# Scores of a pair of heads on the two row halves of TensorE, issued together every second step

## The reference

```
h = rmsnorm(x); proj = h @ w_in
# group A: 8 heads, 2 kv heads, window 128, a learned sink per head
s = einsum(q, k) * 64 ** -0.5;  s = where(0 <= qpos - kpos < 128, s, -inf)
p = softmax(concat(s, sink))[..., :-1];  o_A = p @ v
# group B: 8 heads, 2 kv heads: compressed + selected + window branch, each with its own K/V
o_B = g0 * o_cmp + g1 * o_sel + g2 * o_win
x = x + concat(o_A, o_B) @ w_out
x = x + peer_ffn(rmsnorm(x));   y = rmsnorm(x)
```

## Time and profile before

| | |
|---|---|
| median of three runs | 1526.71 us |
| the profiled execution | 1529.9 us, of which its span (first to last instruction) 1528.0 us |
| attention stage, first scores to last values | 114.8 to 249.7 us |
| TensorE's mean granted clock over the span | 0.997 of full speed |

### The profile page before, as it was taken

One profiled execution on the slowest core, in us unless ns is written; L12 is line 12 of the kernel. 1 busy time (PEld: TensorE's weight loads), 2 busy tenths in 40 slices (PEclk: granted clock), 3 DMA queues, 4 the chain that ended last, 5 costly groups with the idle time before them and its releaser, 6 DMA issues.

```text
span 1528.0 us, 22468 instructions
## 1 busy us (share of the span) xinstructions
PE 1503.2 (98%) x8379; PEld 1345.0 (88%) x8379; DVE 1226.5 (80%) x2329; ACT 629.1 (41%) x1050; POOL 534.3 (35%) x357
## 2 busy tenths in 40 slices
PE   9999999999999999999999999999999999999997
PEld 6888888889899999998888888999999999999996
DVE  5577885449999999975776776888888889888885
ACT  6247675332222356663333333333333333333335
POOL 0323102055755710002111112555555556555530
PEclk9999999999999999999999999999999999999999
DMA  8302003323323668889999989999999999999971
GB/s 313 146 25 87 1 2 128 117 89 112 131 60 114 173 208 307 320 307 368 299 309 301 302 293 339 363 367 370 356 361 370 362 371 361 369 367 356 371 254 69
DMA packets 148507, 378.94 MB, mean 248 GB/s; under 512 B 11792, under 2 KB 76688, under 8 KB 145456
## 3 DMA queue, kind: packets, MB, share of 16 engines
q1 hardware_dynamic: 100400, 201.84, 38.3%
q0 software_dynamic: 37200, 138.56, 24.5%
q10 hardware_dynamic: 10800, 37.11, 6.6%
HBM read 338.60 MB, written 38.86 MB: 247 GB/s over the span
## 4 chain that ended last, share of the span: by engine, by line
PE 85%; DVE 10%; DMA 2%; ACT 1%; issue 1%; SPq 0%; DVEq 0%; ACTq 0%
PE bank L1898 22%; PE bank L1803 20%; PE bank L1524 12%; PE bank L1904 11%; PE bank L1812 10%; PE bank L1735 2%; DVE oh L1406 2%; DVE gp L1414 2%; DVE gp L1411 2%; DVE oh L1409 2%; PE bank L1719 1%; DVE d_lo L1395 1%; DMA w_raw<-wts 1%; PE bank L1644 1%; PE bank L1821 1%
## 5 line engine op out<-in xcount | busy, mean ns | idle before, releaser
L1803 PE MATMUL bank<-h_hi,d_hi 128*128 128x384 f32 x1024 | 349.2, 341 | 1.1 <-DVE h_lo L1260 1.1
L1803 PE MATMUL bank<-h_lo,d_hi 128*128 128x384 f32 x1024 | 344.9, 337 | 0.0
L582 POOL DMA_INDIRECT p_in<-rows,p_row x128 | 160.5, 1254 | 403.7 <-DVE p_dot L1433 186.0
L582 POOL DMA_INDIRECT p_in<-up,p_row x128 | 172.0, 1344 | 191.5 <-DVE p_dot L1433 97.1
L1812 PE MATMUL bank<-h_hi,d_lo 128*128 128x384 f32 x1024 | 200.2, 338 | 0.0
L1803 PEld LDWEIGHTS bank<-h_hi,d_hi 128*128 128x128 f32 x1024 | 192.5, 188 | 4.0 <-issue 1.3
L1803 PEld LDWEIGHTS bank<-h_lo,d_hi 128*128 128x128 f32 x1024 | 192.4, 188 | 3.2
L1898 PE MATMUL bank<-u_hi,w_hi_e 128*128 128x512 f32 x750 | 192.2, 392 | 1.3 <-DVE w_lo_e L1458 1.3
L1898 PE MATMUL bank<-u_hi,w_lo_e 128*128 128x512 f32 x750 | 191.0, 390 | 0.0
L1904 PE MATMUL bank<-u_lo,w_hi_e 128*128 128x512 f32 x750 | 190.8, 390 | 0.0
L1812 PEld LDWEIGHTS bank<-h_hi,d_lo 128*128 128x128 f32 x1024 | 180.8, 188 | 0.0
(11 more groups left out here) (290 smaller groups left out, 2438.8 us busy)
## 6 DMA issues: line engine op xcount, KB each, us to landing
d_raw<-down SPq DMA_DIRECT2D x128, 512.0 KB, 5.7
u_raw<-up SPq DMA_DIRECT2D x128, 512.0 KB
gates_dram<-ev ACTq DMA_DIRECT2D x12, 2048.0 KB, 6.7
g_e<-gates_dram SPq DMA_DIRECT2D x32, 768.0 KB
w_raw<-wts SPq DMA_DIRECT2D x9, 2048.0 KB, 8.3
act_dram<-f_act ACTq DMA_DIRECT2D x59, 192.0 KB
a_e<-act_dram SPq DMA_DIRECT2D x59, 192.0 KB
xt<-x_in SPq DMA_DIRECT2D x2, 2048.0 KB, 11.1
```

The lines of the kernel that those rows point to most:

```text
L582: pool.indirect_dma_start(out=p_in[n % GR][:], out_offset=None, in_=rows if kind == "D" else up.rearrange("n p d -> (n p) d"), in_offset=b ...
L1803: nc.tensor.matmul(bank[6 + e % 2][:, 0:TD], d_hi[e % DH_R][:, k], h[:, k, 0:TD], start=(k == j == 0), stop=False)
```

## The change

Three things change, in one loop of PE and in the order of heads.

1. **Row halves.** A score matmul of up to 256 keys takes only its group's 64 rows of query and key tile (`own`): rows 0 to 63 for group 0, rows 64 to 127 for group 1. In the compiled program these 64 instructions are then placed on a tile of 64 x 128 of the array, 32 of them at row 0 and 32 at row 64. The number of instructions stays the same, and so do the wide scores' operands.
2. **Order of heads.** `UNITS` lists heads 0, 4, 1, 5, 2, 6, 3, 7, so that units 2p and 2p + 1 are the same `j` of both groups. `nmax` and `rsum` keep their columns by head (`column(s)`), so that the sinks and gates still match.
3. **Two at a time.** PE calls `query_keys` for s and s + 1 in even steps, for all widths, and for none in odd steps.

```diff
-UNITS = [(qb, br, h) for qb in range(TB) for br in (SWA, SEL, WIN) for h in range(HEADS)]
+PAIRED = [g * HPG + j for j in range(HPG) for g in range(GROUPS)]
+UNITS = [(qb, br, h) for qb in range(TB) for br in (SWA, SEL, WIN) for h in PAIRED]
+
+
+def column(s):
+
+    return s // HEADS * HEADS + UNITS[s][2]
...
-                                         bias=nmax[:, s:s + 1], accum_out=rsum[:, s:s + 1])\
+                                         bias=nmax[:, column(s):column(s) + 1], accum_out=rsum[:, column(s):column(s) + 1])\
...
-                elif br == SWA:
-                    q = (q_g1 if g else qT)[:, 0, j, tok]
-                else:
-                    q = q_g1[:, 1, j, tok] if g else q_g0[:, j, tok]
+                own = slice(DH * g, DH * g + DH)
+                if br == SWA:
+                    q = (q_g1 if g else qT)[own, 0, j, tok]
+                elif n <= PACKED:
+                    q = q_g1[own, 1, j, tok] if g else q_g0[own, j, tok]
                 if s >= 3:
                     pe.wait_ge(S("max_done"), s - 2)
...
-                    m = nc.tensor.matmul(bank[s % 3][:, 0:n], q, kT[:, K_OF[br], k0:k0 + n], start=True, stop=True)
+                    m = nc.tensor.matmul(bank[s % 3][:, 0:n], q, kT[own, K_OF[br], k0:k0 + n], start=True, stop=True)
...
-                    query_keys(s)
+                    if s % GROUPS == 0:
+                        for u in range(s, s + GROUPS):
+                            query_keys(u)
```

More of the change, by code:

```diff
@@ L1172, in _ @@
                                            scalar=nsink[:, h:h + 1] if br == SWA else -NEG,
-                                           op0=ALU.add, op1=ALU.min, accum_out=nmax[:, s:s + 1])\
+                                           op0=ALU.add, op1=ALU.min, accum_out=nmax[:, column(s):column(s) + 1])\
                      .then_inc(S("max_done"), 1)
@@ L1726, in _ @@
                     gi = u // HEADS
-                    if uh == 0 and gi >= 2:
+                    if u % HEADS == 0 and gi >= 2:
                         pe.wait_ge(S("o_free"), gi - 1)
-                    if uh == 0 and gi == 1:
+                    if u % HEADS == 0 and gi == 1:
                         pe.wait_ge(S("gexp_done"), TB)
```

## The result

Five runs of the changed kernel took 1532.69, 1552.95, 1553.55, 1554.24 and 1554.87 us, median 1553.55, against 1526.71 for the kernel before. The ratio, over runs of both kernels, is 1.0152 (95% interval 1.0108 to 1.0196). The interval is wide because the kernel has two lengths; the profile shown first is of the short one, 1532.69 us, and a second one of 1550 us was taken later.

What follows compares the result with a forecast made beforehand. PE was taken to bound the 137 to 216 us stretch, with DVE close beside it. 16 pairs x 0.20 us, half lost to DVE in eight, give 2.4: 1526.7 - 2.4 = 1524.3 us, full range 1519.8 to 1530.3.

Steps and rivals of the forecast that it cites:

- The pair: 256-key scores of two heads, 137.4 to 215.9 us: side by side, 0.78 us with tile changes against 0.98, 0.20 less.
- The sum: 16 pairs on the path x 0.20 = 3.2 us, cut for DVE to 2.4 us less; 128-key scores gain nothing.
- half of eight pairs: About 8 of 16 pairs lie in or beside 148.2 to 167.6 us, DVE 90% full; they keep 0.10 us each.
- The even step's added wait: PE waits for the maximum of unit s - 2; 0 to 0.4 us per stall, taken as offset by earlier odd-head scores.
- the clock rival: Half-filled arrays and gaps make PE's clock fall once more under PE-bound steps: 1527.7 us, twice 1531.1; chance 0.06.
- such a stretch: 6.8 us at 0.50 of full clock, as from 119.0 to 125.8 us before, doing 3.4 us of work.
- the signs of being wrong: Four records one after another, step pair under 1.9 us, `max_done` stalls before even scores, or clock falling outside 119 to 126 us.

Runs made afterwards that it cites:

- order_only: The changed kernel with full 128-row score matmuls again, keeping pairs and head order; 1524.87 us, ratio 0.9988 to the kernel before.
- fill_start_after: The changed kernel plus six full-array 512-column matmuls in PE's pauses of steps 3 to 5; median 1545.27 us over eleven runs.
- rows_256: The changed kernel with half rows only for 256-key scores, 128-key scores on full rows; two groups, 1523.47 to 1524.71 and 1534.10 to 1536.25 us, ratio 1.0009.
- pause_tiles: Paired order, full-row scores, ten ACT copies pausing PE, and a 64-row matmul of 16 keys ahead of each short pair; 1565.70 us.

## Why the prediction was wrong

- **The pair: right.** Two steps at 2.01 us (forecast 2.00) and the halves side by side. Held against order_only's rows, the changes of tile show on both sides: 0.48 us instead of 0.40 from the values to the pair and 0.28 instead of 0.21 from the transposes to the values, so with the 0.63 us of the pair itself 0.78, as forecast. Here the Trainium skill's rule that matmuls start strictly in program order (TensorE: Matmul & The Clock Gate, part 3) does not hold across row halves, by the four rows above, if each record is an instruction. With its rule on draining at a change of tiling mode (TensorEngine Tiling (Array Packing), Key Properties) the 0.08 and 0.07 us above agree.
- **The sum: near in total, wrong in its parts.** With no fall the changed kernel takes 1523.99 and 1524.91 us (two runs of fill_start_after, with its six added matmuls), 2.3 and 1.4 less than the kernel before in the same series; forecast 2.4 less. That the total comes near is partly luck. For 1.8 us come from the paired order, which I had put at nothing, and some 0.5 from the half rows, which I had put at 2.4 (the runs at 0.998 and above have a median of 1524.4 us in order_only and 1524.0 in rows_256, which is within their spread). Paired, full rows need 2.15 us for two steps, not 2.20, so half rows have only 0.14 us a pair to give; and DVE's waits for these scores fell from 7.1 us to 2.9 by the order alone:

```profile
DVE pr L1179 <- PE bank L1653: 2.9, 6, 0.7
```

And of these 0.14 us a pair most turned into waiting, less for DVE, to which the forecast gave half of eight pairs, than for ACT's exponentials ahead of the transposes. (In fill_start_after DVE is busy 17.30 of the 19.40 us from 148.2 to 167.6, 89%; over 90% was forecast.) Between 137.4 and 215.9 us this wait is, in order_only and then in rows_256:

```profile
PEld bank L1730 <- ACT pr L772: 4.3, 7, 1.2
PEld bank L1730 <- ACT pr L772: 8.2, 16, 1.2
```

- **The even step's added wait: no cost found.** With full rows that order is faster than the one before.
- **The step that failed: the clock rival.** I had named half-filled arrays and gaps at this place, and gave them 0.06 and the price of "such a stretch", once or twice: 1527.7 or 1531.1. But I had the clock fall once more, and in both profiles of the changed kernel it fell once, where it had before, and stayed down. I took the length of 6.8 us at half clock for a property of the clock. It depends on the work that follows: back after 7 us with full rows, after 31 and 79 us in the two profiles of the changed kernel, and 82 us after PE resumed where it was made to pause. The price of one such microsecond was 0.28 to 0.34 us, less than the 0.5 that I had used, but there were 30.7 and 78.5 of them where I had counted with 6.8 or twice that: 8.7 us in the short run and 26.6 in the long one, over the 1522.1 us of the run without a fall. The range ended at 1530.3 for want of this term. Of the signs of being wrong that I had named, the last one came: half clock outside of 119 to 126 us.
- **What starts the fall** stays open, and so does what about the work delays the return (changes of tile, half rows, or how much PE streams). In the changed kernel 8 of 9 runs took 1550 us or more; full-array work in PE's pauses at the start of the stage left 9 of 11 runs with lowered clock.

## What to carry to other kernels

Before changing the shape of matmuls, look in PEclk for a place where the clock falls and returns, and ask what the new matmuls do to the return: a microsecond at half clock cost 0.3 us here, where a pair of heads gained at most 0.19 (2.20 to 2.01). Where PE alternated between a half tile and the full array every microsecond or two, a fallen clock came back only 27 to 106 us later, however busy PE's row looked. Half rows from unit 48 on, with wide full-row matmuls between them, did no harm in 11 runs; and an order that hands the next engine two pieces of work at once can be worth more than the shorter matmul.

## What the runs showed of the hardware that was not expected

- Small 64-row matmuls between scores that are all on full rows kept the clock at 0.50 for 56 us after a pause of PE, against 7 us without; doubling the half-row scores between the same changes of tile brought 82 us down to 27.
- PE was busy 28.70 of 28.70 us in such a window (`pause_tiles`, 156.3 to 185.0 us): the busy time of the trace did not tell whether the clock would return.
- The three longest falls, of 78.5, 92 and 105.8 us, all ended at one place of the program, 1.4 to 2.4 us after PE came to four 256-column matmuls on the full array in a row.
- Matmuls on the two row halves start 0.01 us apart though one stands two records later in the program, and each half keeps its own order.
